# Early output products of the dilated layer from step 4, and identity products ahead of three stage ends

## What is computed

```python
def first_block(x, mem, ...):
    mix = jnp.concatenate([attn_o, dn_o], axis=-1) @ w_out      # window attention and gated delta net
    x = x + rms_norm(mix, g_mix_post)
    c = memory_cross_attention(rms_norm(x), rms_norm(mem), ...)  # ends with  o @ w_o   (stage w_co)
    x = x + rms_norm(c, g_cross_post)
    f = swiglu(rms_norm(x), w_gate_up, w_down)                   # stage ffn_down
    return x + rms_norm(f, g_ffn_post)

def second_block(x, c, ...):
    h = x + 0.5 * gt * swiglu(modulate(rms_norm(h), sh, sc), ...)   # stage ffn_1
    y = dilated_mixer(modulate(rms_norm(h), sh, sc), ...)           # stages dilated, dilated_out
    h = h + gt * y
    ...                                                             # ffn_2, shared keys, ffn_3, sparse mixer, ffn_4

def dilated_mixer(u, w_qkv, q_gain, k_gain, w_o):
    # 3 dilation rates, 16 heads of 64: q, k, v; banded causal attention for each rate;
    # a softmax over the rates weighs the three outputs; then
    return o.reshape(b, s, N_HEADS * HEAD_DIM) @ w_o
```

## Time and profile before

| what | value |
|---|---|
| three timed runs | 3808.28, 3812.08, 3814.58 us; median 3812.08 |
| profiled execution | 3804.64 us, of which the span from the first to the last instruction is 3802.9 us |
| busy share of the span | PE 95%, weight loads into PE 77%, DVE 51%, ACT 38%, POOL 3% |
| mean granted clock of PE | 0.978 (1 is 2.4 GHz, 0.5 is 1.2 GHz) |
| ends of w_co, ffn_down and ffn_1 | at about 771, 1157 and 1546 us |
| last call of the dilated layer | about 2206 to 2264 us |

### The profile page before, as it was taken

The page is one execution under the profiler, slowest core; times in us unless marked ns, Lnnn a source line. Parts: engine busy times, 40 slices in busy tenths (PEclk is TensorE's granted clock), DMA queues, the critical chain, the costliest instruction groups (busy, mean ns, idle before and its releaser), DMA issues.

```text
span 3802.9 us, 50067 instructions
## 1 busy us (share of the span) xinstructions
PE 3621.9 (95%) x19324; PEld 2946.7 (77%) x19324; DVE 1925.5 (51%) x3902; ACT 1436.0 (38%) x2538; POOL 107.4 (3%) x183
## 2 busy tenths in 40 slices
PE   7989989999999999999999989999899998889999
PEld 6779976788887888777777768888788886678887
DVE  5856746555455545555555544333433345764333
ACT  3251132432233222465556543223332234863222
POOL 0000001010001000000000000000000000000000
PEclk9999999999998999999999989999999999999999
DMA  6200036235543554211111212232223221012222
GB/s 243 95 1 1 1 128 226 89 121 176 187 147 125 192 177 146 81 67 51 51 51 50 73 54 89 89 111 89 90 83 117 72 75 45 2 45 89 87 91 78
DMA packets 47161, 359.77 MB, mean 95 GB/s; under 512 B 5217, under 2 KB 5601, under 8 KB 28129
## 3 DMA queue, kind: packets, MB, share of 16 engines
q1 hardware_dynamic: 23472, 269.31, 19.4%
q0 software_dynamic: 23472, 87.50, 6.9%
HBM read 354.69 MB, written 2.10 MB: 94 GB/s over the span
## 4 chain that ended last, share of the span: by engine, by line
PE 84%; DVE 8%; issue 3%; ACT 3%; DVEq 1%; DMA 0%; PEld 0%; ACTq 0%; PEldq 0%; POOL 0%; SPq 0%; POOLq 0%
PE bank L843 22%; PE bank L848 21%; PE bank L849 21%; PE bank L1679 5%; PE bank L2012 1%; PE bank L2029 1%; PE bank L2000 1%; PE bank L984 1%; PE bank L2485 1%; PE bank L2452 1%; DVE w_lo_sb L1280 1%; PE bank L1988 1%; PE bank L805 1%; PE bank L823 1%; PE bank L2474 1%
## 5 line engine op out<-in xcount | busy, mean ns | idle before, releaser
L843 PE MATMUL bank<-x_hi_sb,w_hi_sb 128*128 128x512 f32 x2936 | 1174.4, 400 | 59.6 <-DVE x_lo_sb L1422 15.7
L849 PE MATMUL bank<-x_hi_sb,w_lo_sb 128*128 128x512 f32 x2936 | 1151.4, 392 | 0.0
L848 PE MATMUL bank<-x_lo_sb,w_hi_sb 128*128 128x512 f32 x2936 | 1151.1, 392 | 0.0
L843 PEld LDWEIGHTS bank<-x_hi_sb,w_hi_sb 128*128 128x128 f32 x2936 | 555.5, 189 | 211.5 <-issue 66.1
L1103 ACT ACTIVATE w_hi_sb<-slab_sb 128x1024 fp32r<-128x1024 f32 (+2 forms) x555 | 507.1, 937 | 499.4 <-PE bank L843 312.0
L1280 DVE TENSOR_TENSOR w_lo_sb<-slab_sb,w_hi_sb 128x1024 fp32r<-128x1024 f32 (+2 forms) x555 | 580.8, 1078 | 187.4 <-ACT w_hi_sb L1103 172.2
L849 PEld LDWEIGHTS bank<-x_hi_sb,w_lo_sb 128*128 128x128 f32 x2936 | 555.0, 189 | 119.6
L848 PEld LDWEIGHTS bank<-x_lo_sb,w_hi_sb 128*128 128x128 f32 x2936 | 556.1, 189 | 109.2
L1446 DVE TENSOR_TENSOR hid_sb<-silu_gate_sb,bank 128x512 f32<-128x512 f32 x110 | 75.6, 687 | 602.1 <-PE bank L849 602.1
L843 PE MATMUL bank<-hid_hi_sb,w_hi_sb 128*128 128x512 f32 x880 | 342.8, 390 | 0.0
L849 PE MATMUL bank<-hid_hi_sb,w_lo_sb 128*128 128x512 f32 x880 | 342.6, 389 | 0.0
(11 more groups left out here) (361 smaller groups left out, 3742.4 us busy)
## 6 DMA issues: line engine op xcount, KB each, us to landing
slab_sb<-weights SPq DMA_DIRECT2D x79, 2048.0 KB, 7.9
keep_sb<-ada POOLq DMA_DIRECT2D x133, 512.0 KB, 4.5
slab_sb<-weights SPq DMA_DIRECT2D x44, 1536.0 KB, 6.5
slab_sb<-weights SPq DMA_DIRECT2D x20, 1280.0 KB, 6.0
tables_sb<-ada POOLq DMA_DIRECT2D x14, 512.0 KB, 6.2
work_sb<-ada POOLq DMA_DIRECT2D x13, 512.0 KB, 8.0
h_sb<-x SPq DMA_DIRECT2D x4, 512.0 KB, 6.7
out<-h_sb SPq DMA_DIRECT2D x8, 256.0 KB, 2.0
```

The costliest lines, as they stand in the source:

```text
L843: mm = pe.matmul(out, w_hi[p][:, w], hi, start=first, stop=False)
L848: pe.matmul(out, w_hi[p][:, w], lo, start=False, stop=False)
L849: return pe.matmul(out, w_lo[p][:, w], hi, start=False, stop=last)
```

## The change

- `pe_dilated`: early products begin behind step 4 instead of step 7; so 18 of the 21 stand behind steps and 3 behind the last one, where it was 15 and 6.
- `act_dilated`, `dve_dilated`: the split of weight part 0 of the output projection moves from the beginning of the last call to the end of the call before it (`if last`); the `out_tile` calls of the last call move forward in both lists.
- `pe_run`: 25 identity products ahead of the stage ends of w_co, ffn_down and ffn_1.

```diff
@@ -2074,7 +2074,7 @@
                 assert e.single[1].pos % 4 == OUT_SEAT, "the outputs begin in the projections' banks"
                 for m in range(22):
                     between(m)
-                    if m >= 7:
+                    if m >= 4:
                         early_product()
                         at += 1
                 while at < 3 * (KT - 1):
@@ -2161,26 +2161,24 @@
             if attending:
                 act_root_rows(e, tp, e.tp, rows_dilated)
                 values_turned(2)
-            out_part(0)
-            out_tile(0)
+            out_tile(0, 1, 2)
             swap_in(0, 0)
             w_hi_part(4)
             exp(0)
-            out_tile(1, 2)
+            out_tile(3)
             swap_in(0, 1)
             w_hi_part(5)
             exp(1)
+            out_tile(4)
             turned(0, 0)
-            out_tile(3)
+            out_tile(5)
             value_tile(0)
             turned(0, 1)
-            out_tile(4)
+            out_tile(6)
             w_hi_part(6)
             turned(0, 2)
-            out_tile(5)
             exp(2)
             turned(1, 0)
-            out_tile(6)
             out_part(1)
             swap_in(1, 0)
             w_hi_part(7)
@@ -2219,6 +2217,8 @@
             act.activation(root, root, ACT.Sqrt, scale=1.0 / HALF, bias=small[:, 120:121]).then_inc(rooted, 1)
             act_table(e, ACT.Exp)
             w_hi_part(14)
+            if last:
+                act_w_hi(e, 0, D)
 
         def dve_dilated(e, par, first=False, last=False, project=True, attending=True):
             dve = e.eng
@@ -2310,26 +2310,24 @@
                     k = d_qk[old][g][1]
                     tt(k, k, e.S.bank[s][:, :], ALU.mult).then_inc(e.S.free[s], 1)
                 dve.drain().then_inc(heads_ready, 1)
-            out_part(0)
+            out_tile(0, 1)
             mask(0)
+            out_tile(2)
             rope(0, 0)
             w_lo_part(4)
-            out_tile(0)
             weigh(0)
-            out_tile(1)
+            out_tile(3)
             mask(1)
+            out_tile(4)
             w_lo_part(5)
             rope(0, 1)
             keep_sums(0)
             value_tile()
-            out_tile(2)
             weigh(1)
-            out_tile(3)
+            out_tile(5, 6)
             mask(2)
             w_lo_part(6)
-            out_tile(4, 5)
             weigh(2)
-            out_tile(6)
             out_part(1)
             mask(3)
             rope(1, 0)
@@ -2360,6 +2358,8 @@
             dve.tensor_scalar(d_inv[par][:, 0:24], d_inv[par][:, 0:24], 0.125, None, ALU.mult)
             dve_root_parts(e, d_inv[par][:, 24:48].rearrange("p (g b x) -> p b g x", g=3, b=NB), 3, 2)
             w_lo_part(14)
+            if last:
+                dve_w_lo(e, 0, D)
 
 
         n_kslc = cut(keep, 0, 4, S)
@@ -2626,6 +2626,7 @@
             pe_stay_busy(e, 20)
             pe_linear_parts(e)
             pe_sums_open(e, crosses[0])
+            pe_stay_busy(e, 25)
             e.stage_end("w_co")
             pe_stay_busy(e, 4)
             pe_sums_close(e, crosses[0])
```

## The result

The median of the changed kernel is 3826.04 us over seven runs (3824.12 to 3829.89). The kernel before, run beside it on the same chip, has a median of 3809.28 (3807.60 to 3814.58). 3826.04 lies within 1 us of the forecast of 3827.0. The profiled execution of the changed kernel took 3826.62 us (span 3824.8, granted clock 0.978).

The account below looks back on a forecast made before the run. PE bounds the kernel (84% of the span on its chain), though path scores bound the dilated call's first part. Ends +8.3 and dilated call +6.6 make +14.9, added to the median 3812.08: 3827.0 us, range 3815 to 3833.

Parts of the forecast that it names:

- The sum: Whole kernel: +8.3 for the three stage ends and +6.6 for the dilated call, together +14.9 us.
- w_co, +4.2: End of w_co: 25 uncovered products cost 7.2, faster clock returns 2.3 and 0.7; +4.2 us, ends +2.1 and +6.1.
- ffn_down, +1.4: End of ffn_down: products cost 6.3 beyond PE's wait, clock returns 4.0 and 0.9; +1.4 us, ends -2.0 and +4.0.
- PE's clock is at 1.2 GHz when they start, so 25 x 0.336 = 8.4: End of ffn_down: the 25 identity products run slowly at 0.336 us each, 8.4 us, of which 2.09 is covered.
- The lower bound of the prediction, -2.0: End of ffn_down: products at 0.232 us each and everything given back by the clock would make -2.0 us.
- ffn_1, +2.7: End of ffn_1: products 5.8 less PE's wait of 1.6, clock returns 1.5; +2.7 us, ends +2.7 and +4.2.
- The dilated call, +6.6: Last call of the dilated layer: late scores and masks less three products fewer at the end; +6.6 of +2.8 to +7.3 us.
- product 4 waits for x_lo 4: Dilated call, step 8: PE waits about 3 us for x_lo 4, ready about 2232.0, ahead of scores(2,0).
- mask(3)'s delay: Dilated call: mask(3) starts at 2247 to 2251.5 instead of 2242.05, 4.9 to 9.4 us later, behind product 7's wait.
- The clock pays back in full: Rival at the three stage ends: they cost +2.8 instead of +8.3, in sum +9.4, 3821.5 us; chance 0.17.
- Not slower: Rival at dilated steps 8 to 11: inputs ready, tail shorter, -2.1; with ends at +2.8, +0.7, 3812.8 us; chance 0.13.
- The change does not do what it says: Rival in the dilated call: products released when they were before, only the ends count, +8.3, 3820.4 us; chance 0.10.

Follow-up runs that it names:

- behind the end: Kernel before with the 25 identity products just behind each of the three stage ends instead of ahead, dilated layer as before: 3823.64 us, ratio 1.0032.
- the products alone: Kernel before with 25 identity products ahead of the ends of w_co, ffn_down and ffn_1, dilated layer as before: 3819.90 against 3810.80 us, ratio 1.0023.
- nine products alone: Kernel before with 9 identity products ahead of the end of ffn_down, 7 at ffn_1, none at w_co: 3809.78 against 3810.45 us, ratio 0.9999.
- the inputs alone: Kernel before with the change's early products, their copies, subtractions and second weight part made sooner, product order unchanged: 3811.82 against 3810.27 us, ratio 1.0005.
- the run from step 7 on: Changed kernel without identity products, early products back at step 7, moved copies, subtractions and weight split kept: 3810.57 us, ratio 1.0002 against the kernel before.

## Why the prediction was right, step by step

**The sum.** Forecast +14.9, measured +16.8 between the medians. The forecast was put on the median of three runs, 3812.08; over seven it is 3809.28. So the base was 2.8 too high and the sum 1.9 too small, and the two errors cancel to 1 us. That it is so close is luck; the places below are off by up to 2.7.

**w_co, +4.2; measured +4.1 in the change, +4.0 behind the end, +5.7 with the products alone.** The +5.7 is too much: in that profile PE stood at the lower level sooner, and against three untouched ends where it did so too (36.35 us, last section) it is +4.3. All terms held: 7.2 for the products (7.45 measured, 8.58 in the run with the products alone), -2.3 back from the one-column row (-2.4), -0.7 from the spread (-0.7). That nothing covers them shows in ACT's wait, 7.3 us longer, as foreseen.

**ffn_down, +1.4; measured -1.3.** The term that failed is "PE's clock is at 1.2 GHz when they start, so 25 x 0.336 = 8.4": they took 5.84, 2.6 us less, which is nearly all of the difference of 2.7. The stretch of those products stands at 1.00 of the clock (columns as above):

```profile
1162.20:1167.90 5.70, 5.70 (x50) 5.57 (x50) 1.29 (x2) 1.24 (x2) 0.00 (x0) 1.00 0.01 3
```

In the kernel before, the clock had fallen already ahead of the wait: PE's last product there took 0.57 us (1154.37, granted clock 0.59 from 1154.30 to 1154.95), in the changed kernel 0.40 (1161.62). With nine products alone the clock was at 0.65 in their row, 0.378 us each, so there the prediction's 1.2 GHz was nearer. At which level the products start differs between executions, and so does the end without them: 36.88 to 39.04 us in the eight profiles. Whether this end loses or gains is not settled (-1.3 to +0.8). The lower bound of the prediction, -2.0, was worked out with the right duration.

**ffn_1, +2.7; measured +3.9.** The products cost 5.84 (5.8 foreseen). The cover was taken at the full 1.60 of PE's wait, but 0.66 of it stays idle; and the two rows behind gave back 0.3 and 0.8 instead of 1.5 together. 5.84 - 0.94 - 1.1 = +3.8. In the eight profiles the untouched end takes 22.44 to 23.83 us; in the four shorter ones (22.4) the two rows behind it take 1.02 and 1.16 us without any products, as short as behind the 25, so what came back here depends on the execution.

**The dilated call, +6.6; measured +7.5.** Counted from L745, at 2208.09 before (the root turn ahead of the earlier trace rows) and at 2215.89 after:

| step | predicted | measured |
|---|---|---|
| opening | some 0.7 later | 0.66 (scores(0,0)) |
| product 4 waits for x_lo 4 | about 3 us | 2.68 us |
| scores(2,0) run at | 25.1 to 26.0 | 26.1 |
| mask(2) later by | 2.4 to 4.3 | 3.7 |
| second weight part ready at | 35.9 to 37.9 | 37.95 (2252.62 + 1.22) |
| product 7 waits for it | about 5 us | 4.82 us |
| mask(3) later by | 4.9 to 9.4 | 9.4 |
| end, three products fewer | -2.1 | -2.16 (4.67 to 2.51) |

The waits and their order came as written. The mis-sized term is mask(3)'s delay, taken at 8.7 of 4.9 to 9.4 (+6.6 and the 2.1 of the end): it came at the upper end in both its parts. The weight part is ready at 37.95, and mask(3) starts 5.4 us behind that, of 3.0 to 5.5 foreseen. 9.4 - 2.1 = +7.3 of the 7.5. One place was misread: of products 0 to 3, which were all put into PE's idle time ahead of scores(1,1), two run ahead of scores(1,0), which starts 1.8 us later than before; scores(1,1) starts only 0.3 later, so no cost came of it.

Behind its idle time of 4.82 us PE runs at the lower level, while it had stood above it before:

```profile
2243.00:2248.00 5.00, 5.00 (x32) 2.64 (x30) 2.93 (x12) 1.07 (x2) 0.00 (x0) 0.83 0.00 0
...
2254.00:2257.50 3.50, 3.50 (x15) 2.23 (x15) 0.00 (x0) 0.00 (x0) 0.00 (x0) 0.50 0.00 0
```

**The rivals.** "The clock pays back in full" would be +2.8 for the ends; +8.8 (5.0 to 12.2) was measured, and w_co alone costs about +4 in three profiles. That the clock does come up behind denser work agrees with the rule cited in the prediction from the Trainium skill, TensorE: Matmul & The Clock Gate, Part 1 (activity releases the throttled clock): 5.12 to 2.74 us for the same 24 records. It is a return, not a full refund. "Not slower" put its point at 2.1 us of waiting for both inputs together; the two are 7.5. "The change does not do what it says" falls with the waits ahead of L843.

## What to carry to other kernels

Before work is moved forward in an in-order queue, put the time at which its inputs come beside the time at which the queue gets there: everything behind the moved instruction inherits the difference, and here two products ahead of the scores cost more than three products at the end gave back. Move the inputs first, then order the products as the inputs come: that turned +7 us into -8, where the inputs alone gave no gain. Filler products for the clock did not pay here: as many as roughly fit into PE's waits cost and gained nothing that can be told, and where PE arrives last at a stage end 25 of them cost about 4 us after what the clock gave back, on either side of the end.

## What the hardware showed that was not expected

**The same code at two clock levels from one execution to the next.** A stretch that no edit touches, 64 products of 62 columns, in the kernel before and in the changed one:

```profile
2711.25 7.34 PE L2692 MATMUL bank<-work_sb,slab_sb 128*128 128x62 f32 x64
2718.85 1.97 PE L735 MATMUL bank<-const_sb,small_sb 128*64 128x128 f32 x32 [0.26 <-issue]
```
```profile
2727.39 12.09 PE L2695 MATMUL bank<-work_sb,slab_sb 128*128 128x62 f32 x64
2739.74 3.55 PE L735 MATMUL bank<-const_sb,small_sb 128*64 128x128 f32 x32 [0.26 <-issue]
```

The granted clock was 1.00 in the first (2711.3 to 2718.5) and 0.58 in the second (2727.4 to 2739.4), while PE had been busy 10.62 of the 11 us ahead of it in both, at a clock of 1.00. In the profiles of the eleven experiments the row takes 12.06 to 13.88 us; only that of the kernel before shows 7.34. These two rows make 6.3 of the 21.9 us by which the two spans differ, so the spans overstate the change, and the medians (16.8) are what counts. It may also be why the profiled execution of before lay 7.4 us under the median of its first three runs. What sets the level there was not found.

**The same at w_co, ahead of any edit.** The one-column products ahead of the end of w_co, in the run with the identity products alone and in the run from step 7 on:

```profile
774.12 3.31 PE L990 MATMUL bank<-const_sb,work_sb 128*128 128x1 f32 x24 [0.47 <-issue]
```
```profile
768.49 3.30 PE L990 MATMUL bank<-const_sb,work_sb 128*128 128x1 f32 x24 [0.47 <-issue]
```

In the kernel before and in the changed one the row takes 2.81 us. The granted clock was 1.00 in it before (768.21 to 771.01) and 0.88 in the run from step 7 on (768.49 to 771.29), and PE had been busy 4.53 of the 5 us ahead of it in both, at 1.00. Of the eight kernels whose three ends are as before, five show 2.81: their end of w_co takes 34.9 us, the products behind it 349.8, the end of ffn_down 39.0. Three show 3.30 to 3.32: there the same stretches take 36.4, 352.8 and 36.9. The 25 products of w_co took 7.45 us in the changed kernel and 8.58 in the run with the products alone, which began with the slower row. So differences of 1 to 3 us at one place of one profile are within what the clock does from one execution to the next; what sets it was not found.
